# Making one more of a weight chunk's block sums with an accumulating DMA instead of VectorE, in a one-core decoder layer on Trainium2

## The reference

```python
def swiglu(x, wg, wu, wd):
    return (jax.nn.silu(x @ wg) * (x @ wu)) @ wd

h = layer_norm(DN_ALPHA * h + 0.5 * swiglu(h, ffn1_wg[l], ffn1_wu[l], ffn1_wd[l]), ln1_g[l], ln1_b[l])
mix = token_mixer(h, w_in[l], ...)
h = layer_norm(DN_ALPHA * h + mix, ln2_g[l], ln2_b[l])
h = layer_norm(DN_ALPHA * h + 0.5 * swiglu(h, ffn2_wg[l], ffn2_wu[l], ffn2_wd[l]), ln3_g[l], ln3_b[l])
```

## Time and profile before

| | before |
|---|---|
| median of three runs | 2176.2 us (2175.06 to 2176.49) |
| the profiled execution, own time | 2173.46 us |
| its span in the trace | 2171.7 us |
| TensorE busy | 98% of the span |
| VectorE, ScalarE busy | 80%, 60% |
| mean granted TensorE clock | 0.995 of 2.4 GHz |
| bytes moved by DMA | 508.17 MB |

### The profile page before, as it was taken

How to read it: one execution, slowest core, us unless ns; L and a number is a source line. 1 busy time by engine, 2 the same in 40 slices (tenths; PEclk the granted TensorE clock), 3 DMA queues, 4 the chain that set the end, 5 groups by cost and what they waited for, 6 DMA issues and landing times.

```text
span 2171.7 us, 25619 instructions
## 1 busy us (share of the span) xinstructions
PE 2136.9 (98%) x9556; PEld 1771.3 (82%) x9556; DVE 1734.4 (80%) x1438; ACT 1310.4 (60%) x1303; POOL 169.9 (8%) x281
## 2 busy tenths in 40 slices
PE   8999999999999999999999999998999999999997
PEld 6888888888887888888888888886888888888886
DVE  7799999999977567677776465658899999999986
ACT  5677777777752544454545344434677777777761
POOL 0111111111010000000000000000111111101110
PEclk9999999999999999999999999999999999999999
DMA  8688888888764555555455555555678888898862
GB/s 349 233 289 273 272 268 282 264 284 298 259 242 146 203 205 172 173 185 186 153 173 192 193 196 188 217 204 203 232 233 272 269 269 293 289 301 276 291 249 85
DMA packets 97372, 508.17 MB, mean 234 GB/s; under 512 B 13440, under 2 KB 13824, under 8 KB 56704
## 3 DMA queue, kind: packets, MB, share of 16 engines
q1 hardware_dynamic: 81216, 433.50, 54.0%
q0 software_dynamic: 16064, 73.42, 15.4%
HBM read 493.23 MB, written 13.63 MB: 233 GB/s over the span
## 4 chain that ended last, share of the span: by engine, by line
PE 95%; DVE 2%; DMA 1%; ACT 0%; issue 0%; SPq 0%; POOL 0%; DVEq 0%; ACTq 0%
PE acc L1635 11%; PE acc L1634 11%; PE acc L1633 11%; PE acc L1696 11%; PE acc L1698 11%; PE acc L1697 11%; PE tb L1698 9%; PE tb L1697 9%; PE tb L1696 9%; PE tb L1681 1%; DMA g_raw<-in_groups 1%; DVE g_lo L1030 1%; DVE act_sb L1296 0%; DMA raw<-in_stream 0%; PE tb L1957 0%; PE tb L1971 0%
## 5 line engine op out<-in xcount | busy, mean ns | idle before, releaser
L1030 DVE TENSOR_TENSOR g_lo<-g_raw,g_hi 128x2048 fp32r<-128x2048 f32 x370 | 837.9, 2284 | 120.9 <-ACT g_hi L637 120.3
L637 ACT ACTIVATE g_hi<-g_raw 128x2048 fp32r<-128x2048 f32 x370 | 706.5, 1916 | 263.1 <-PE acc L1698 82.8
L1007 DVE TENSOR_TENSOR w_lo<-raw,w_hi 128x1024 fp32r<-128x1024 f32 x272 | 326.9, 1220 | 170.7 <-ACT w_hi L597 167.3
L597 ACT ACTIVATE w_hi<-raw 128x1024 fp32r<-128x1024 f32 x272 | 279.0, 1057 | 165.0 <-PE acc L1635 99.4
L1633 PE MATMUL acc<-w_hi,xT_hi 128*128 128x512 f32 x768 | 302.2, 393 | 0.0
L1635 PE MATMUL acc<-w_hi,xT_lo 128*128 128x512 f32 x768 | 299.4, 390 | 0.0
L1634 PE MATMUL acc<-w_lo,xT_hi 128*128 128x512 f32 x768 | 299.2, 390 | 0.0
L1696 PE MATMUL acc<-g_hi,xF_hi 128*128 128x512 f32 x696 | 273.3, 393 | 15.4 <-DVE g_lo L1383 9.1
L1697 PE MATMUL acc<-g_lo,xF_hi 128*128 128x512 f32 x696 | 272.0, 391 | 0.0
L1698 PE MATMUL acc<-g_hi,xF_lo 128*128 128x512 f32 x696 | 272.0, 391 | 0.0
L1696 PE MATMUL tb<-g_hi,xF_hi 128*128 128x512 f32 x568 | 221.0, 389 | 0.0
(11 more groups left out here) (148 smaller groups left out, 2866.1 us busy)
## 6 DMA issues: line engine op xcount, KB each, us to landing
g_raw<-in_groups SPq DMA_DIRECT2D x262, 1024.0 KB, 7.0
raw<-in_stream SPq DMA_DIRECT2D x272, 512.0 KB, 4.4
g_raw<-in_groups POOLq DMA_DIRECT2D x48, 1024.0 KB, 8.0
bounce<-h_sq POOLq DMA_DIRECT2D x44, 256.0 KB, 4.9
h_in<-bounce POOLq DMA_DIRECT2D x176, 64.0 KB, 2.7
ln_gb<-in_ln SPq DMA_DIRECT2D x6, 1024.0 KB, 5.3
g_raw<-in_groups SPq DMA_DIRECT2D x4, 512.0 KB, 7.6
res<-in_x_rows SPq DMA_DIRECT2D x1, 2048.0 KB, 16.4
```

The costliest lines, as they stand in the source:

```text
L597: act.activation(w_hi[:, seg.split(j)], raw[:, seg.raw(j)], ACT.Copy).then_inc(hi_ready, 1)
L637: act.activation(g_hi[:, n % RING], source[:], ACT.Copy).then_inc(g_hi_ready, 1)
L1007: dve.tensor_tensor(w_lo[:, s], raw[:, seg.raw(j)], f32(w_hi[:, s]), ALU.subtract).then_inc(lo_ready, 1)
L1030: dve.tensor_tensor(g_lo[:, n % RING], source[:], f32(g_hi[:, n % RING]), ALU.subtract).then_inc(g_lo_ready, 1)
```

## The change

T4b, the last of the sums in `qb`, is made by an accumulating DMA on POOL's queue. VectorE's `add` for it goes, together with its waits. The buffer of `gb` is still loaded by SP, since P2b needs it; the DMA reads the same group from HBM a second time. POOL's new DMA waits until P6b, which uses the old content of `qb`, is split; ScalarE waits for the DMA before it splits P4b.

```diff
@@ -82,7 +82,7 @@
-FULL_SUMS = ("T1a", "T3a", "T2a", "T2b", "T4b")
+FULL_SUMS = ("T1a", "T3a", "T2a", "T2b")
@@ -344,6 +344,7 @@
+        t4b_ready = sem("t4b_ready")
@@ -785,7 +786,8 @@
                 split_loaded(f, b, "D4", "D4")
                 empty(f, b, "D3")
-                split_sum(f, b, "P4b", "qb", "T4b")
+                act.wait_ge(t4b_ready, fulls(f, b))
+                split(f, b, "P4b", "qb")
@@ -1158,9 +1160,6 @@
                 lo_group(f, b, "P7b", "rb")
                 lo_group(f, b, "D3", "D3")
-                load_done(f, b, "gb")
-                split_done(f, b, "P6b")
-                add(qb, qb, gb)
                 lo_group(f, b, "P4a", "qa")
                 lo_group(f, b, "P2a", "ga")
@@ -1615,6 +1614,8 @@
                         pool.wait_ge(g_lo_ready, lo_count(G.at[f, b + 1, "P6a"]))
                         add_from_hbm(f, b + 1, "qa", "ga", t4a_ready)
+                        pool.wait_ge(g_lo_ready, lo_count(G.at[f, b + 1, "P6b"]))
+                        add_from_hbm(f, b + 1, "qb", "gb", t4b_ready)
```

More of the change, by code:

```diff
@@ L1132, in full_block @@
             def full_block(f, b):
-                qa, qb, ra, ua, ub, gb = (source(f, b, name) for name in ("qa", "qb", "ra", "ua", "ub", "gb"))
+                qa, qb, ra, ua, ub = (source(f, b, name) for name in ("qa", "qb", "ra", "ua", "ub"))
                 lo_group(f, b, "P1a", "qa")
```

## The result

The changed kernel takes 2194.93 us (median of 4 runs, 2191.89 to 2198.33) against 2175.96 us before: ratio 1.0088, 95% interval 1.0076 to 1.0100. It is 19 us slower, as forecast to the microsecond.

A forecast was written before the change was run, and what follows sets the result against it. TensorE bounds the kernel, waiting for nothing in full chunks. Waits of 0.9 us a chunk (14 us), raised to 1.2 by carried lateness, give 16 x 1.2 = 19 us on the median 2176.2: 2195, range 2179 to 2213.

The forecast's parts named there:

- VectorE's relief is worth nothing: In the full chunks, taking sixteen sums (36.6 us) off VectorE gains nothing, as TensorE waits for neither neighbouring split.
- The DMA engines are the place, by lateness against a room and not by bytes: Around D3, the new DMA delays loads; TensorE waits only for lateness beyond the room, 0.66 to 1.86 us at D3.
- the 0.96 of the sum: DMA engines' share of a full chunk's 60 us, forecast to rise from 0.88 to 0.96.
- T4b's own price: Each new accumulating DMA of 1.05 MB takes 4.9 us of all sixteen DMA engines.
- hidden by the free 12%: Rival: 7 us of 60 free on the DMA engines hide the new DMA's 4.9; 2176, up to 2180; chance 0.19.
- D3 is 2.3 us late: D3's load, its last 0.44 MB moving beside T4b, takes 3.3 us for them, not 1.0: 2.3 us late.
- mean 0.9: TensorE's wait at D3, lateness less room: 1.05, 0.47, 1.64, 0.44 us in four chunks, mean 0.9; 14 us over sixteen.
- P2a: 0.4 us, covered by D3's wait: At P2a, ga's load comes 4.9 us later; the split ends 0.4 us late, which D3's wait covers.
- What it leaves behind: a third of it, 0.3 us a chunk: After P2a, VectorE's lateness carries over, about 1 us; a third taken raises the wait to 1.2 us a chunk.
- Whole pieces: Rival: DMA engines change queues only after whole groups, so only ga is 4.9 us late; 2182; chance 0.10.
- Cascade: Rival: lateness grows from chunk to chunk, 2.5 us a chunk or more; 2216 and up; chance 0.12.
- P4b late for T4b: Sign of being wrong: TensorE waits at P4b for the new semaphore, so T4b is late and not the loads.

The follow-up runs named there:

- the kernel without the sum: Changed kernel with the new DMA removed and T4b made by no engine: 2175.49 us, 1.0003 over the kernel before.
- the two halves: Changed kernel with T4b's DMA split into two of 0.5 MB, one behind P6b's split, one behind D3's: 2177.53 us, 1.0008 over the kernel before.
- the alternating kernel: Changed kernel with the DMA making T4b in even full chunks only (8 of 16), VectorE in odd ones: 2180.84 us, 1.0026 over the kernel before.
- no T2b: Changed kernel with VectorE's sum T2b not made and all DMAs kept: 2194.45 us, 1.0084 over the kernel before.
- two halves in place: Changed kernel with T4b as two DMAs of 0.5 MB, both behind P6b's split: 2200.70 us, 1.0117 over the kernel before.

## Why the prediction was right, point by point

*VectorE's relief is worth nothing.* Shown by the kernel without the sum.

*The DMA engines are the place, by lateness against a room and not by bytes.* Shown: half of the time costs 0 and the whole 19 us; the same bytes cost 19, 20, 1 and 25 us behind P6b, P7a, P7b and D3, each against the kernel before on its chip. The share around the chunk measured 0.92, not the 0.96 of the sum. Part of the difference is the longer period, but not all: over eight chunks it is 0.86 before and 0.92 behind P7b, where the period is unchanged, 0.06 more and not 0.08. T4b's own price was right (5.2 us, expected 4.9); the loads' packets took 1.6 us a chunk less than before. The rival "hidden by the free 12%" is true of the place behind P7b, and of the two halves.

*D3 is 2.3 us late.* The load took 2.0 us more in the mean of sixteen chunks, of which not all is direct: in the alternating kernel it is 11.7 against about 9.9, 1.8. The step was right. Its price was not: "mean 0.9" a chunk was the term of waits, and the direct wait in a chunk whose forerunner has no such DMA measured 0.45 us with P2a's included. Two things made it too large. The four chunks that I took for the sixteen have a mean room of 1.4 us; all sixteen of the trace before have 0.4 to 3.2, 1.8 in the mean. And I took one lateness for all of them. Before, D3's load takes 7.8 to 11.3 us, longest where the room is smallest; after, it takes 11.2 to 12.4 everywhere. So it is 3.7 and 3.8 us longer in the two full chunks where both the room is longest and the load shortest, and 1.1 in the one with the shortest room. Where the room is small, D3's load has less left when T4a ends (landing 0.3 us behind T4a's at 1801.90, 0.9 at 1742.06).

*P2a: 0.4 us, covered by D3's wait.* Undersized: with D3 spared (behind P7a) it alone cost the whole 19 us. ga was late by 4.6 to 5.0 us in the chunks shown and 4.9 in the mean, as in the sum; but behind P7a ga's load is itself issued 0.5 us late in the mean, and then this room is gone too. D3 and P2a have nearly the same room left: sparing D3 altogether (the place behind P7a) brought nothing, and easing it (no T2b, or two halves in place) moved the waits to P2a.

*What it leaves behind: a third of it, 0.3 us a chunk.* Undersized: 0.95 - 0.45 = 0.50. D3's load was issued 1.0 us late in the chunk worked out, which is what the step gave ("about 1 us"), and 0.5 in the mean of sixteen; the choice of a third of the extra wait was too low. The two errors, -0.45 and +0.2 a chunk, leave 0.95 where the sum had 1.2. In sixteen chunks that is 15.3 us and not 19, and 3.1 us that the sum had left out lie outside the full chunks, 1.8 of them in the two chunks behind. So the total agrees to the microsecond by luck; the path (the DMA engines, D3's late load, a wait of TensorE for its split) is as forecast. The profiled execution, from which these parts come, is also the fastest of four, 3 us under the median.

*Whole pieces* is refuted: with it D3 would not have been late. The packet counts show turns by rows, which is half and half in bytes as long as the rows of both sides have 8 KB. *Cascade* didn't come: the loss a chunk doesn't grow along a network, and in the changed kernel D3's load is never issued more than 1.0 us late; that TensorE's waits give the others their time back is the likely reason, but no run shows it alone. *P4b late for T4b*: TensorE waits for P4b in no trace; behind D3's split the DMA landed 10 to 15 us after D3 started, in most chunks only 5 to 7 us before P4b began.

*Left open:* what carries lateness over when ga is the late load. VectorE's stretch from P2a to P3a is one carrier; removing a sum from it cured D3's issue and not the total.

## What to carry to other kernels

Taking work off an engine that nobody waits for pays nothing, and giving it to the DMA engines may cost: first ask which load is just in time, and what the new transfer will be beside. The same 1 MB cost 0.9% or nothing according to whether its wait stood 8 us earlier or later, so try a new transfer at several places before judging it. When two loads have nearly the same room, curing one shows the other. And a hit of the sum proves little: lay the traces side by side and check each term.

## What was not expected of the hardware

The DMA engines take turns between SP's and POOL's queues by rows, and not by whole groups or by bytes: in 3 us the loads moved 0.39 MB beside an accumulation with rows of 8 KB, and 0.57 MB beside one with rows of 4 KB. An accumulating DMA of half the size (rows of 4 KB) beside loads with rows of 8 KB lengthened D3's load by 0.7 us in the mean, a plain copy of full size by 1.0, the whole accumulation by 2.0; two halves in a row again by only 0.7 (10.6 us, although ga was 5 us late). The size of a row, and not only the bytes in the queue, sets how a load fares beside another queue.
